# Head of a transformer block on Trainium2: conditioning groups summed on TensorE as columns, and the first projection units begun inside the head

## The chip, the cores and the metric

The kernel runs on one core of one Trainium2 chip. The metric is the device time of the whole kernel in microseconds (us). A core has TensorE (PE; its weight loads are shown as PEld), VectorE (DVE), ScalarE (ACT), GpSimd (POOL) and SyncE (SP), which here only issues DMAs. The engines run their own instruction streams and wait for one another on semaphores.

## The reference

The block has two sub-layers. What is touched here is the very beginning of the first one. Shapes: x is (512, 1024), c is (1, 1024), w_ada is (1024, 6144), w_in is (1024, 9 thousand odd columns), all float32.

```python
ada = (jax.nn.silu(c) @ w_ada[l] + b_ada[l])[:, None, :]
shift1, scale1, gate1, shift2, scale2, gate2 = jnp.split(ada, ADA_PARTS, axis=-1)
h = rms_norm(x, g_pre_mix[l]) * (1.0 + scale1) + shift1
# hybrid_mixer begins with one projection, whose first columns are convolved
proj = h @ w_in
m_qk = jax.nn.silu(causal_depthwise_conv(m_qk, conv_w, conv_b))
...
x = x + gate1 * rms_norm(y, g_post_mix[l])
# sub-layer 2: product-key retrieval over 16384 experts
```

## The kernel before, in words

All matrix products are done with a weight matrix split into two parts, a rounded part (`whi`, type fp32r) and the rest (`wlo`), and the activations too (`hi`, `lo`), three products for each pair. `h` is kept transposed: 8 slices k of 128 channels by 512 tokens.

**The head** (`head_block`, lines 143 to 374) makes `hi` and `lo` of the first sub-layer. It needs the first 2048 columns of `silu(c) @ w_ada` (shift1 and scale1). They come in 8 column groups of 256 columns, 1 MB each, in 4 pairs p: group p (shift) and group 4 + p (scale); each pair serves two slices k = 2p and 2p + 1. Groups 0 to 3 are summed by TensorE (`dot_columns`, line 248): silu(c) is the stationary operand of one column, the weights are the moving one of 256 columns, and the result is one row, which ACT copies out of PSUM (line 308) and TensorE turns into two columns (`turn_columns`, line 264). Groups 4 to 7 are summed by DVE in 8 steps (`ada_columns`, lines 135 and 138) and then turned by TensorE in the same way (line 264). A float32 matmul appears as two records in the trace, a transpose as one. Then DVE adds the bias (line 352) and makes the scale (line 356), ACT writes h and `hi` of both slices from the transposed x (lines 314 and 316, two instructions for each slice), and DVE writes `lo` (line 336). x itself is squared and summed by ACT (line 300), normalised by DVE (line 331) and transposed by TensorE (line 270, four transposes for each slice). The DMA queue of SP carries, in this order: small rows, x (2 MB), more small rows, the eight w_ada groups, and two groups of w_in (`load_ahead`, line 395).

Engines take their work strictly in program order, and the order is written out by hand. A block ends when all engines have finished it.

**The first projection** (`project_block`, called as "proj_m") runs over 18 groups of 256 weight columns. For a group, DVE casts the raw weights to `whi` (line 561), POOL subtracts to get `wlo` (line 488) and TensorE makes two units of 128 columns by 512 tokens, each 8 slices times 3 products = 24 matmuls (line 534). The very first group is an exception: its `whi` and `wlo` are made by DVE in four pieces at the start of the block (lines 579 and 581), and its first unit follows piece by piece. DVE convolves each of the first 16 units (lines 686 and 691), four instructions for a unit, and it casts the weights for the next group in between. Units of the later sections are emptied by ACT or DVE. SP loads groups two ahead, as soon as the raw buffer is free (line 451).

Of the kernel before, what the change touches and what calls it, by code (L numbers as in the profile page):

```python
# [79 lines left out]
HBUF = 4  # L80

# [37 lines left out]
def as_f32(ap):  # L119
    return ap.bitcast(F32)  # L120
# [22 lines left out]
def head_block(nc, con, slots, A, x_src, hi, lo):  # L143
# [3 lines left out]
    pairs_of, by_pe = [(p, KD // 2 + p) for p in range(KD // 2)], (0, 1, 2, 3)  # L147
    order = [g for pair in pairs_of for g in pair]

    with Alloc(nc, "head") as al:  # L150
# [7 lines left out]
        row = [al.sb(f"row{i}", [1, GC]) for i in range(2)]  # L158
# [4 lines left out]
        ps_t = al.ps("ps_t", [P, 512])  # L163
        ps_row = [al.ps(f"ps_row{i}", [P, 512]) for i in range(2)]
        ps_u = ps_l = ps_t
        ps_ada = al.ps("ps_ada", [P, 512])
# [6 lines left out]
        x_in = [al.sem(f"x_in{i}") for i in range(NT // 2)]  # L173
        acc_step, summed_up, ada_done, scale_done, lam_in, lam_prod, lam_sum, lam_exp, lam_done = map(
            al.sem, ("acc_step", "summed_up", "ada_done", "scale_done", "lam_in", "lam_prod", "lam_sum", "lam_exp",
                     "lam_done"))
        summed, meaned, powed, normed, turned, modded, hi_done, lo_done, row_done, row_kept = map(
            al.sem, ("summed", "meaned", "powed", "normed", "turned", "modded", "hi_done", "lo_done", "row_done",
                     "row_kept"))
        in_turn = [g for g in order if g in by_pe]  # L180
        row_turned = [order.index(g) + 1 for g in in_turn]
        block = al.block()

        @block.sync
        def _(sp):
            def rows(dst, r, src, n, sem):
                sp.dma_start(dst[r:r + n, :], src.rearrange("(r p) -> r p", p=P)).then_inc(sem, 16)

            rows(rows_a, R_BADA, A["b_ada"][0], 48, rows_in)
            rows(rows_a, R_GPREMIX, A["g_pre_mix"][0], 8, rows_in)  # L190
            rows(rows_a, R_GPOSTMIX, A["g_post_mix"][0], 8, rows_in)
            rows(rows_a, R_GPREFFN, A["g_pre_ffn"][0], 8, rows_in)
            rows(rows_a, R_GPOSTFFN, A["g_post_ffn"][0], 8, rows_in)
            rows(rows_a, R_CONVB, A["conv_b"][0], 16, rows_in)
            rows(rows_a, R_C, A["c"][0], 8, rows_in)
            for t in range(NT):
                sp.dma_start(x[:, t], x_src[t * P:(t + 1) * P, :]).then_inc(x_in[t // 2], 16)
            rows(rows_b, R_CONVW, A["conv_w"][0].rearrange("w c -> (w c)"), 64, rows_b_in)
            rows(rows_b, R_MGAIN, A["m_head_gain"][0], 8, rows_b_in)
            rows(rows_b, R_DGAIN, A["d_head_gain"][0], 8, rows_b_in)  # L200
            for n, name in enumerate(("lam_q1", "lam_q2", "lam_k1", "lam_k2")):
                sp.dma_start(con.lam_cols[:, n:n + 1], A[name].rearrange("a p -> p a")).then_inc(lam_in, 16)

            for n in range(2):
                sp.dma_start(con.gate_bias[:, n:n + 1],
                             A["b_if"][:, n * HEADS:(n + 1) * HEADS].rearrange("a h -> h a")).then_inc(lam_in, 16)
            for g in order[:-2]:
                sp.dma_start(raw[:, g], A["w_ada"][g].rearrange("p (k n) -> p k n", k=KD)).then_inc(landed[g], 16)
            for half, sems in enumerate(([landed[g] for g in order[-2:]], late)):
                ks = slice(half * KD // 2, (half + 1) * KD // 2)  # L210
                for g, sem in zip(order[-2:], sems):
                    src = A["w_ada"][g].rearrange("p (k n) -> p k n", k=KD)[:, ks]
                    sp.dma_start(raw[:, g, ks], src).then_inc(sem, 16)
            slots.load_ahead(sp, w_group(A["w_in"][0], C_QK))

        @block.gpsimd
        def _(pool):
# [13 lines left out]
            pool.tensor_tensor(rstd[:], ms[:], con.pow_half[:, 0:NT], ALU.pow).then_inc(powed, 1)  # L231
        @block.tensor
        def _(pe):
            pe.wait_ge(consts, 7)
            pe.wait_ge(rows_in, 112)
            pe.transpose(ps_t[:, 0:NROWS_A], rows_a[:], con.ident[0:NROWS_A, 0:NROWS_A]).then_inc(a_turned, 1)

            vec = [g for g in order if g not in by_pe]

            def dot_columns(g):  # L240

                i = in_turn.index(g)
                pe.wait_ge(landed[g], 16)
                wait(pe, row_kept, i - 1)
                for k in range(KD):
                    if k == KD // 2 and g in order[-2:]:
                        pe.wait_ge(late[order[-2:].index(g)], 16)
                    mm = pe.matmul(ps_row[i % 2][0:1, 0:GC], con.silu_c[:, k:k + 1], raw[:, g, k, :], start=(k == 0),
                                   stop=(k == KD - 1))
                mm.then_inc(row_done, 1)  # L250

            def turn_columns(g):

                if g in by_pe:
                    i = in_turn.index(g)
                    pe.wait_ge(row_kept, i + 1)
                    src, one, inner = row[i % 2], con.ones[0:1, 0:1], slice(0, 1)
                else:
                    i = vec.index(g)
                    pe.wait_ge(acc_step, KD * (i + 1))  # L260
                    src, one, inner = acc[i % 2], con.ones[:, 0:1], slice(0, P)
                for m in range(GC // P):
                    c = g * GC // P + m
                    mm = pe.matmul(ps_ada[:, c:c + 1], src[inner, m * P:(m + 1) * P], one, start=True, stop=True)
# [9 lines left out]
            for p, pair in enumerate(pairs_of):  # L274
                if p == 1:
                    pe.wait_ge(rows_b_in, 48)
                    pe.transpose(ps_u[:, 0:NROWS_B], rows_b[:], con.ident[0:NROWS_B, 0:NROWS_B]).then_inc(b_turned, 1)
                if p == 2:
                    pe.wait_ge(lam_prod, 1)
                    pe.wait_ge(cols_ready, 2)  # L280
                    pe.matmul(ps_l[:, 0:2], con.ones[:], sq[:], start=True, stop=True).then_inc(lam_sum, 1)
                for g in pair:
                    if g in by_pe:
                        dot_columns(g)
                if p == 0:
                    pe.wait_ge(normed, NT)
                for k in (2 * p, 2 * p + 1):
                    turn(k)
                for g in pair:
                    turn_columns(g)  # L290
        @block.scalar
        def _(act):
            act.wait_ge(cols_ready, 1)
            act.activation(con.silu_c[:], con.cols_a[:, R_C:R_C + KD], ACT.Silu).then_inc(silu_ready, 1)
            for t in range(NT):
                act.wait_ge(x_in[t // 2], 32)
# [4 lines left out]
            n_pe = 0  # L301
            for p, pair in enumerate(pairs_of):
                for g in pair:
                    if g in by_pe:
                        act.wait_ge(row_done, n_pe + 1)
                        if n_pe >= 2:
                            act.wait_ge(summed_up, row_turned[n_pe - 2])
                        act.activation(row[n_pe % 2][:], ps_row[n_pe % 2][0:1, 0:GC], ACT.Copy).then_inc(row_kept, 1)
                        n_pe += 1
# [8 lines left out]
                if p == 2:  # L318
                    act.wait_ge(lam_sum, 1)
                    act.activation(esum[:], ps_l[:, 0:2], ACT.Exp).then_inc(lam_exp, 1)  # L320

        @block.vector
        def _(dve):
# [6 lines left out]
            for t in range(NT):  # L330
# [2116 lines left out]
```

## Time and profile before

| | us |
|---|---|
| median of 3 runs | 2013.84 |
| lowest and highest | 2013.56, 2015.16 |
| span of the profiled execution | 2011.3 |

| engine | busy us | share of the span |
|---|---|---|
| PE | 1937.0 | 96% |
| DVE | 1489.4 | 74% |
| ACT | 719.0 | 36% |
| POOL | 481.5 | 24% |

The span runs from the first to the last instruction; what lies around it makes the 2.5 us to the median. Idle time of an engine that is not the bottleneck costs nothing; what an engine waited for is put down to the releaser that came last. PEclk is the TensorE clock that was granted, 1.00 for 2.4 GHz and 0.50 for 1.2 GHz. Matmuls are pipelined, so one record can be longer than the distance to the next one.

### The profile page before, as it was taken

What the parts mean: (1) busy time and instruction counts of PE and PEld (TensorE: products, weight loads), DVE (VectorE), ACT (ScalarE), POOL (GpSimd) and SP (SyncE); (2) the same over time, 40 slices, a digit from 0 to 9 for tenths busy, and PEclk for the clock granted to TensorE, in tenths of its full rate; (3) what the DMA queues carried; (4) which work ended last, traced back from release to release, by engine and by line L of the source; (5) the groups of instructions that cost most, each with busy time, mean ns of one, the idle gap of its engine ahead of it and who ended that gap; (6) DMA issues with size and microseconds to landing.
All of it is one profiled execution on the core that took longest, in us unless ns stands there. A gap on an engine that the chain in (4) does not pass through costs nothing.

```text
span 2011.3 us, 27895 instructions
## 1 busy us (share of the span) xinstructions
PE 1937.0 (96%) x10341; PEld 1714.5 (85%) x10341; DVE 1489.4 (74%) x2727; ACT 719.0 (36%) x1324; POOL 481.5 (24%) x240
## 2 busy tenths in 40 slices
PE   5999998999999989999999999999999999999998
PEld 3889776889877888899999999999988888888886
DVE  5677445364475545787889999997689889899895
ACT  4110234010252243344443444444444444444443
POOL 0443202343213113100111521111222323332221
PEclk9999999999999999999999999999999999999999
DMA  6335511354212422257767688888999999999993
GB/s 253 105 106 182 172 54 48 106 191 147 63 43 73 158 80 88 72 173 255 234 225 241 231 318 297 299 296 300 412 395 401 401 400 398 400 398 401 400 375 115
DMA packets 212642, 467.99 MB, mean 233 GB/s; under 512 B 13576, under 2 KB 157120, under 8 KB 193344
## 3 DMA queue, kind: packets, MB, share of 16 engines
q1 hardware_dynamic: 194112, 332.54, 47.6%
q0 software_dynamic: 18432, 134.23, 16.9%
q8 instruction: 51, 0.84, 0.2%
q14 instruction: 47, 0.39, 0.1%
HBM read 412.19 MB, written 54.53 MB: 232 GB/s over the span
## 4 chain that ended last, share of the span: by engine, by line
PE 52%; DVE 2%; DMA 2%; ACT 1%; issue 0%; POOLq 0%; POOL 0%; SPq 0%; ACTq 0%; DVEq 0%
PE xin_out L2038 26%; PE xin_ps_u L1994 22%; PE xin_out L2016 4%; DMA con_raw<-in_expert_u 2%; DVE in_ulo L2156 1%; ACT in_uhi L2067 0%; DVE experts_rows L1787 0%; DVE experts_acc L1806 0%; DVE over_s_stage L2170 0%; ACT L2109 0%; ACT over_v_vhi L2074 0%; DVE over_v_vlo L2305 0%; POOLq L95 0%; POOL xin_x L2147 0%; DVE over_s_stage L2253 0%
## 5 line engine op out<-in xcount | busy, mean ns | idle before, releaser
L1780 POOL DMA_INDIRECT experts_rows<-in_expert_rows,experts_idx x128 | 247.3, 1932 | 873.2 <-DVE experts_acc L1806 738.4
L1994 PE MATMUL xin_ps_u<-con_h_hi,in_uhi 128*128 128x384 f32 x1024 | 349.0, 341 | 9.4 <-DVE in_ulo L2156 7.2
L1994 PE MATMUL xin_ps_u<-con_h_hi,in_ulo 128*128 128x384 f32 x1024 | 343.3, 335 | 0.0
L1994 PE MATMUL xin_ps_u<-con_h_lo,in_uhi 128*128 128x384 f32 x1024 | 343.3, 335 | 0.0
L2038 PE MATMUL xin_out<-over_v_vhi,xin_whi 128*128 128x512 f32 x768 | 239.1, 390 | 2.1 <-DVE xin_wlo L2307 2.0
L2038 PE MATMUL xin_out<-over_v_vhi,xin_wlo 128*128 128x512 f32 x768 | 238.8, 390 | 0.0
L2038 PE MATMUL xin_out<-over_v_vlo,xin_whi 128*128 128x512 f32 x768 | 238.5, 390 | 0.0
L2156 DVE TENSOR_TENSOR in_ulo<-con_raw,in_uhi 128x1024 fp32r<-128x1024 f32 x127 | 155.5, 1224 | 78.3 <-ACT in_uhi L2067 75.9
L488 POOL TENSOR_TENSOR weights_wlo<-con_raw,weights_whi 128x2048 fp32r<-128x2048 f32 x32 | 147.5, 4609 | 251.9 <-DVE weights_whi L561 251.9
L1994 PEld LDWEIGHTS xin_ps_u<-con_h_hi,in_uhi 128*128 128x128 f32 x1024 | 193.1, 189 | 13.7 <-DVE in_ulo L2156 11.1
L1994 PEld LDWEIGHTS xin_ps_u<-con_h_lo,in_uhi 128*128 128x128 f32 x1024 | 193.2, 189 | 0.0
L1994 PEld LDWEIGHTS xin_ps_u<-con_h_hi,in_ulo 128*128 128x128 f32 x1024 | 192.7, 188 | 0.0
L2038 PEld LDWEIGHTS xin_out<-over_v_vhi,xin_whi 128*128 128x128 f32 x768 | 144.0, 188 | 33.4 <-DVE over_v_vlo L2305 2.7
L2074 ACT ACTIVATE over_v_vhi<-con_raw 128x1024 fp32r<-128x1024 f32 x128 | 135.0, 1055 | 103.8 <-DMA con_raw<-in_expert_v 88.6
L2092 ACT ACTIVATE in_act<-xin_ps_u 128x384 f32<-128x384 f32 x128 | 62.9, 491 | 300.2 <-PE xin_ps_u L1994 300.2
L2038 PEld LDWEIGHTS xin_out<-over_v_vhi,xin_wlo 128*128 128x128 f32 x768 | 144.3, 188 | 29.9
L2038 PEld LDWEIGHTS xin_out<-over_v_vlo,xin_whi 128*128 128x128 f32 x768 | 144.3, 188 | 29.7
L2305 DVE TENSOR_TENSOR over_v_vlo<-con_raw,over_v_vhi 128x1024 fp32r<-128x1024 f32 x128 | 156.4, 1222 | 9.1 <-ACT over_v_vhi L2074 8.8
L1806 DVE SCALAR_TENSOR_TENSOR experts_acc<-experts_rows,experts_coef,experts_acc 128x1024 f32<-128x1024 f32 x127 | 162.8, 1282 | 0.1
L1787 DVE SCALAR_TENSOR_TENSOR experts_rows<-experts_rows,con_h 128x1024 f32<-128x1024 f32 x128 | 156.3, 1221 | 0.1
L2067 ACT ACTIVATE in_uhi<-con_raw 128x1024 fp32r<-128x1024 f32 x127 | 133.9, 1054 | 9.3 <-DMA con_raw<-in_expert_u 9.0
L2076 ACT ACTIVATE xin_whi<-xin_wt 128x384 fp32r<-128x384 f32 x128 | 67.2, 525 | 177.7 <-DVE xin_wt L2302 177.2
(344 smaller groups left out, 3742.4 us busy)
## 6 DMA issues: line engine op xcount, KB each, us to landing
con_raw<-in_expert_u SPq DMA_DIRECT2D x128, 512.0 KB, 4.7
con_raw<-in_expert_v SPq DMA_DIRECT2D x128, 512.0 KB, 12.0
con_raw<-in_w_in SPq DMA_DIRECT2D x38, 1024.0 KB, 6.0
act_scratch<-in_act SPq DMA_DIRECT2D x128, 192.0 KB, 2.4
experts_hot<-act_scratch SPq DMA_DIRECT2D x128, 192.0 KB, 11.8
gate_scratch<-in_stage SPq DMA_DIRECT2D x12, 1024.0 KB, 7.1
gate_scratch<-over_s_stage SPq DMA_DIRECT2D x12, 1024.0 KB, 7.7
experts_hot<-gate_scratch SPq DMA_DIRECT2D x16, 768.0 KB, 14.1
```

The costliest lines, as they stand in the source:

```text
L488: pool.tensor_tensor(wlo[s][:], raw[s][:], as_f32(whi[s][:]), ALU.subtract).then_inc(w_lo, 1)
L1780: pool.indirect_dma_start(out=self.rows[:, r % ROWS, :], out_offset=None, in_=table, in_offset=at).then_inc(self.row_in[r % ROWS], 16)
L1787: dve.scalar_tensor_tensor(out=u, in0=u, scalar=1.0, in1=h0, op0=ALU.mult, op1=ALU.mult, accum_out=self.dots[:, r:r + 1]).then_inc(self.do ...
L1806: dve.scalar_tensor_tensor(out=self.acc[:], in0=v, scalar=self.coef[:, r:r + 1], in1=self.acc[:], op0=ALU.mult, op1=ALU.add).then_inc(self ...
L1994: mm = pe.matmul(ps_u[s % 2][:, 0:TD], a[s % 2][:, k, :], m[:, k, P:T], start=(i == 0), stop=(i == 3 * KD - 1))
L2016: mm = pe.matmul(ps_g[b][:, k, :], hot_j[q % 2][:, 4 * b + k, :], hot_i[q % 2][:, 4 * b + k, :], start=True, stop=True)
L2038: product = lambda s, t, h, w, m, **flags: pe.matmul(out[t][h][:], w[s][:, t * P:(t + 1) * P], m[s][:, h * 512:(h + 1) * 512], **flags)
L2067: act.activation(uhi[n % 2][:], cut_of[n % U_RING], ACT.Copy).then_inc(hi_done, 1)
L2074: act.activation(vhi[s][:], v[s], ACT.Copy).then_inc(vhi_done, 1)
L2076: act.activation(whi[s][:], wt[n % 2][:], ACT.Copy).then_inc(whi_done, 1)
L2156: dve.tensor_tensor(ulo[n % 2][:], cut_of[n % U_RING], as_f32(uhi[n % 2][:]), ALU.subtract).then_inc(lo_done, 1)
L2305: dve.tensor_tensor(vlo[s][:], v[s], as_f32(vhi[s][:]), ALU.subtract).then_inc(vlo_done, 1)
```

## The change

- `dots(p)` takes the place of `dot_columns` and of the turning of its row: the raw weights (128 x 128) are the stationary operand and one column of silu(c) the moving one; 2 column blocks by 8 slices = 16 matmuls for a group (32 records), straight into columns of PSUM. ACT's copies of the rows (line 308) go.
- The loads: w_ada group 0 goes ahead of x; the first w_in group goes ahead of the last pair of w_ada; the second w_in group stays last. Small rows, lambda columns and gate biases are issued on ACT's queue instead of SP's (three before silu, six behind it). x is waited for tile by tile.
- x: DVE normalises two of the four tiles, ACT the other two. TensorE transposes slices 0 to 3 at once, then 4 and 5, then 6 and 7.
- Both first w_in groups are split in the head: `whi` by ACT (`split_hi`), `wlo` by DVE (`split_lo`), group 0 between pairs 2 and 3, group 1 at the very end. The four-piece split at the start of proj_m goes, and so do DVE's cast and POOL's subtraction of group 1.
- `begin`: units 0 and 1 are begun in the head's two first PSUM banks, with 7 of 8 slices (42 of 48 matmuls), as far as `lo` is done. Four slices of unit 0 stand ahead of `turn_columns(3)` on TensorE. proj_m only adds slice 7.

```diff
+BEGUN, BEGUN_K = 2, 7
...
         @block.sync
...
+            column_group(PAIRS_OF[0][0])
             for t in range(NT):
-                sp.dma_start(x[:, t], x_src[t * P:(t + 1) * P, :]).then_inc(x_in[t // 2], 16)
...
+                sp.dma_start(x[:, t], x_src[t * P:(t + 1) * P, :]).then_inc(x_in[t], 16)
+            column_group(PAIRS_OF[0][1])
+            for pair in PAIRS_OF[1:LAST]:
+                for g in pair:
+                    column_group(g)
+            sp.dma_start(slots.raw[0][:], load_in(sp, 0, 0)).then_inc(slots.landed[0], 16)
+            for half, sems in enumerate(([landed[g] for g in PAIRS_OF[LAST]], late)):
...
+            sp.dma_start(slots.raw[1][:], load_in(sp, 0, 1)).then_inc(slots.landed[1], 16)
...
         @block.tensor
...
-                    mm = pe.matmul(ps_row[i % 2][0:1, 0:GC], con.silu_c[:, k:k + 1], raw[:, g, k, :], start=(k == 0),
-                                   stop=(k == KD - 1))
...
+            def dots(p):
...
+                        mm = pe.matmul(ps_ada[p % 2][:, c:c + 1], raw[:, g, k, m * P:(m + 1) * P],
+                                       con.silu_c[:, k:k + 1], start=(k == 0), stop=(k == KD - 1))
+                mm.then_inc(dotted, 1)
...
+            def begin(c, ks):
+
+                cs = slice(c * P, (c + 1) * P)
+                for k in ks:
+                    pe.wait_ge(lo_done, k + 1)
+                    for n, (a, m) in enumerate(((slots.whi, hi), (slots.whi, lo), (slots.wlo, hi))):
+                        pe.matmul(bank[c][:], a[0][:, k, cs], m[:, k, :], start=(k == 0 and n == 0), stop=False)
+
             pe.wait_ge(silu_ready, 1)
...
+            dots(0)
...
+            pe.wait_ge(normed, NT // 2)
+            pe.wait_ge(act_normed, NT // 2)
+            for k in range(4):
+                turn(k)
+            turn_columns(0)
+            dots(1)
+            turn_columns(1)
...
+            for k in (4, 5):
+                turn(k)
+            dots(2)
+            turn_columns(2)
+            for k in (6, 7):
+                turn(k)
+            dots(3)
+            pe.wait_ge(lam_exp, 1)
+            pe.wait_ge(w_lo, 1)
+            begin(0, range(0, 4))
+            turn_columns(3)
+            begin(1, range(0, 4))
+            for ks in (range(4, 6), range(6, BEGUN_K)):
+                for c in range(BEGUN):
+                    begin(c, ks)
...
         @block.scalar
...
+            act.wait_ge(powed, 1)
+            for t in range(NT // 2, NT):
+                act.activation(x[:, t], x[:, t], ACT.Copy, scale=rstd[:, t:t + 1]).then_inc(act_normed, 1)
+
+            def split_hi(s):
+                act.wait_ge(slots.landed[s], 16)
+                act.activation(slots.whi[s][:], slots.raw[s][:], ACT.Copy).then_inc(w_hi, 1)
+
+            for p in range(LAST + 1):
+                if p == 2:
+                    act.wait_ge(lam_sum, 1)
+                    act.activation(esum[:], ps_l[:, 0:2], ACT.Exp).then_inc(lam_exp, 1)
+                    split_hi(0)
                 act.wait_ge(scale_done, p + 1)
...
+            split_hi(1)
...
         @block.vector
...
+            def split_lo(s):
+                dve.wait_ge(w_hi, s + 1)
+                dve.tensor_tensor(slots.wlo[s][:], slots.raw[s][:], as_f32(slots.whi[s][:]),
+                                  ALU.subtract).then_inc(w_lo, 1)
...
+            sums(1)
+            scales(1)
+            for k in (0, 1):
+                low(k)
+            sums(2)
+            scales(2)
+            for k in (2, 3):
+                low(k)
+            split_lo(0)
+            sums(3)
+            scales(3)
+            for k in (4, 5):
+                low(k)
...
+            for k in (6, 7):
+                low(k)
+            split_lo(1)
+    return bank
...
-def project_block(nc, tag, slots, sections, make, ada=None, following=None, split_first=False):
+def project_block(nc, tag, slots, sections, make, ada=None, following=None, begun=None):
...
-        before = 0 if split_first else 1
-        bank = [al.ps(f"bank{i}", [P, 512]) for i in range(4)]
...
+        before = 2 if begun else 1
+        home = [al.ps(f"bank{i}", [P, 512]) for i in range(4)]
+        bank = begun + home[BEGUN:] if begun else home
...
+                            if begun and opening and s == 0:
+
+                                ks = range(BEGUN_K, KD)
...
-                dve.tensor_copy(whi[0][:, part], raw[0][:, part]).then_inc(hi_sem, 1)
...
-                dve.tensor_tensor(wlo[0][:, part], raw[0][:, part], as_f32(whi[0][:, part]),
-                                  ALU.subtract).then_inc(lo_sem, 1)
```

## Rows read from the trace of the kernel before

**Rows 1.** The page: busy time of each engine, and the chain that ended last.

```profile
PE 1937.0 (96%) x10341; PEld 1714.5 (85%) x10341; DVE 1489.4 (74%) x2727; ACT 719.0 (36%) x1324; POOL 481.5 (24%) x240
PE 52%; DVE 2%; DMA 2%; ACT 1%; issue 0%; POOLq 0%; POOL 0%; SPq 0%; ACTq 0%; DVEq 0%
```

**Rows 2.** Busy us in three stretches: PE, PEld, DVE, ACT, POOL, PEclk, DMA, GB/s.

```profile
42.00:46.00 4.00, 0.00 (x0) 0.00 (x0) 2.73 (x6) 2.93 (x5) 0.00 (x0) 0.50 0.00 0
46.00:52.00 6.00, 4.90 (x12) 3.85 (x13) 5.23 (x9) 1.13 (x1) 0.55 (x1) 0.50 0.11 13
...
18.00:38.00 20.00, 18.43 (x105) 10.24 (x104) 15.91 (x43) 9.00 (x15) 0.00 (x0) 1.00 0.99 372
```

**Rows 3.** Timeline, end of the head: start us, us, engine, line, what, [idle before].

```profile
41.79 0.16 DVE L356 SCALAR_TENSOR_TENSOR con_scale_a<-con_ada,con_cols_a 128x2 f32<-128x2 f32 x1
...
43.99 0.78 ACT L316 ACTIVATE con_h_hi<-head_ps,con_ada,con_scale_a 128x512 fp32r<-128x512 f32 x1
44.87 0.69 DVE L336 TENSOR_TENSOR con_h_lo<-head_h,con_h_hi 128x512 fp32r<-128x512 f32 x1 [0.64 <-ACT con_h_hi L316]
...
45.89 0.43 DVE L579 CAST weights_whi<-con_raw 128x512 fp32r<-128x512 f32 x1 [0.33 <-PEq L95]
...
47.10 0.79 PE L534 MATMUL proj_m_bank<-con_h_hi,weights_whi 128*128 128x512 f32 x1 [5.60 <-DVE weights_wlo L581]
```

**Rows 4.** Timeline, x and the first pair of groups in the head.

```profile
12.58 1.06 ACT L300 ACTIVATE head_junk<-head_x 128x1024 f32<-128x1024 f32 x1
...
14.31 5.35 PE L248 MATMUL head_ps_row<-head_raw,con_silu_c 128*1 128x256 f32 x16 [9.25 <-DMA head_raw<-in_w_ada]
...
15.16 2.74 DVE L331 TENSOR_SCALAR head_x<-head_x,head_rstd 128x1024 f32<-128x1024 f32 x4 [1.15 <-POOL head_rstd L231]
...
18.20 3.61 DVE L138 SCALAR_TENSOR_TENSOR head_acc<-head_raw,con_silu_c,head_acc 128x256 f32<-128x256 f32 x7
...
21.86 0.61 PE L264 MATMUL head_ps_ada<-con_ones,head_acc 128*128 128x1 f32 x4 [0.64 <-DVE head_acc L138]
...
22.77 0.16 DVE L356 SCALAR_TENSOR_TENSOR con_scale_a<-con_ada,con_cols_a 128x2 f32<-128x2 f32 x1
```

**Rows 5.** Groups by line in the head: count, busy us, mean ns.

```profile
L264 PE MATMUL head_ps_ada<-con_ones,head_acc 128*128 128x1 f32 x16 | 2.4, 256 | 0.7 <-DVE head_acc L138 0.6
```

**Rows 6.** Timeline of PE: four transposes twice; and a stretch's granted clock.

```profile
336.71 0.66 PE L880 MATMUL mlstm_ps_t<-con_ident,mlstm_cell 128*128 128x128 f32 x4 [1.14 <-DVE mlstm_cell L957]
338.66 1.05 PE L880 MATMUL mlstm_ps_t<-con_ident,mlstm_cell 128*128 128x128 f32 x4 [1.30 <-DVE mlstm_tmp L963]
...
339.00:340.00 1.00, 0.71 (x4) 0.31 (x2) 0.25 (x1) 0.18 (x1) 0.00 (x0) 0.50 0.00 0
```

**Rows 7.** PE at matmuls of four rows, and the stretch behind them.

```profile
255.90 3.70 PE L834 MATMUL mlstm_ps_n<-mlstm_g,con_sel 4*128 4x512 f32 x8
...
260.30:263.50 3.20, 3.20 (x5) 1.17 (x4) 0.80 (x2) 3.17 (x5) 0.29 (x1) 0.50 0.00 0
```

**Rows 8.** Groups by line of the whole kernel: operations on 128x2048 elements.

```profile
L488 POOL TENSOR_TENSOR weights_wlo<-con_raw,weights_whi 128x2048 fp32r<-128x2048 f32 x32 | 147.5, 4609 | 251.9 <-DVE weights_whi L561 251.9
...
L2233 DVE TENSOR_TENSOR over_s_stage<-over_s_stage 128x2048 f32<-128x2048 f32 x8 | 18.3, 2285 | 0.0
...
L1738 ACT ACTIVATE weights_whi<-con_raw 128x2048 fp32r<-128x2048 f32 x7 | 13.4, 1913 | 2.8 <-PEq L95 1.5 <-DMA con_raw<-in_w_query 1.3
```

**Rows 9.** DMA from 0 to 42 us in 40 slices, and SP's issue of w_in.

```profile
GB/s 0 23 12 16 203 367 417 351 414 346 238 421 421 414 414 437 398 460 414 421 437 414 445 406 414 367 277 250 414 409 381 378 344 352 347 227 33 13 8 0
...
14.21 14.18 SPq L395 DMA_DIRECT2D con_raw<-in_w_in  x2
```

**Rows 10.** Timeline of DVE in proj_m: two convolutions' first steps, a cast between.

```profile
60.61 0.81 DVE L686 TENSOR_SCALAR proj_m_acc<-proj_m_bank,con_cols_b,con_cols_a 128x512 f32<-128x512 f32 x1 [2.27 <-PE proj_m_bank L534]
...
63.70 1.22 DVE L561 CAST weights_whi<-con_raw 128x2048 fp32r<-128x2048 f32 x1
66.05 0.81 DVE L686 TENSOR_SCALAR proj_m_acc<-proj_m_bank,con_cols_b,con_cols_a 128x512 f32<-128x512 f32 x1 [1.14 <-PE proj_m_bank L534]
```

More of the change, by code:

```diff
@@ L143, in head_block @@
 def head_block(nc, con, slots, A, x_src, hi, lo):
-    pairs_of, by_pe = [(p, KD // 2 + p) for p in range(KD // 2)], (0, 1, 2, 3)
-    order = [g for pair in pairs_of for g in pair]
+    PAIRS_OF, LAST = [(p, KD // 2 + p) for p in range(KD // 2)], KD // 2 - 1
+    w_ada_of = lambda g: A["w_ada"][g].rearrange("p (k n) -> p k n", k=KD)
     with Alloc(nc, "head") as al:
@@ L200, in _ @@
[L200 to L208, printed above, removed]
@@ L209, in _ @@
-            for half, sems in enumerate(([landed[g] for g in order[-2:]], late)):
+            rows(sp, rows_a, R_BADA, A["b_ada"][0], 48, rows_in)
+            rows(sp, rows_a, R_GPREMIX, A["g_pre_mix"][0], 8, rows_in)
+            rows(sp, rows_a, R_GPOSTMIX, A["g_post_mix"][0], 8, rows_in)
+            rows(sp, rows_a, R_GPREFFN, A["g_pre_ffn"][0], 8, rows_in)
+            rows(sp, rows_a, R_GPOSTFFN, A["g_post_ffn"][0], 8, rows_in)
+            rows(sp, rows_a, R_CONVB, A["conv_b"][0], 16, rows_in)
@@ L210, in _ @@
+            sp.dma_start(slots.raw[0][:], load_in(sp, 0, 0)).then_inc(slots.landed[0], 16)
+            for half, sems in enumerate(([landed[g] for g in PAIRS_OF[LAST]], late)):
                 ks = slice(half * KD // 2, (half + 1) * KD // 2)
[L211 to L214, printed above, removed]
+                for g, sem in zip(PAIRS_OF[LAST], sems):
+                    sp.dma_start(raw[:, g, ks], w_ada_of(g)[:, ks]).then_inc(sem, 16)
@@ L236, in _, with turn_columns @@
             pe.transpose(ps_t[:, 0:NROWS_A], rows_a[:], con.ident[0:NROWS_A, 0:NROWS_A]).then_inc(a_turned, 1)
-            vec = [g for g in order if g not in by_pe]
-            def dot_columns(g):
-                i = in_turn.index(g)
+            def dots(p):
+                g = PAIRS_OF[p][0]
                 pe.wait_ge(landed[g], 16)
[L244 to L247, printed above, removed]
-                    mm = pe.matmul(ps_row[i % 2][0:1, 0:GC], con.silu_c[:, k:k + 1], raw[:, g, k, :], start=(k == 0),
-                                   stop=(k == KD - 1))
[L250 to L261, printed above, removed]
-                for m in range(GC // P):
-                    c = g * GC // P + m
-                    mm = pe.matmul(ps_ada[:, c:c + 1], src[inner, m * P:(m + 1) * P], one, start=True, stop=True)
+                if p >= 2:
+                    pe.wait_ge(ada_done, 2 * (p - 1))
+                for m in range(GC // P):
+                    for k in range(KD):
+                        if p == LAST and m == 0 and k == KD // 2:
+                            pe.wait_ge(late[0], 16)
+                        c = g * GC // P + m
+                        mm = pe.matmul(ps_ada[p % 2][:, c:c + 1], raw[:, g, k, m * P:(m + 1) * P],
+                                       con.silu_c[:, k:k + 1], start=(k == 0), stop=(k == KD - 1))
+                mm.then_inc(dotted, 1)
+            def turn_columns(p):
+                pe.wait_ge(acc_step, KD * (p + 1))
+                for m in range(GC // P):
+                    c = PAIRS_OF[p][1] * GC // P + m
+                    mm = pe.matmul(ps_ada[p % 2][:, c:c + 1], acc[p % 2][:, m * P:(m + 1) * P], con.ones[:, 0:1],
+                                   start=True, stop=True)
                 mm.then_inc(summed_up, 1)
@@ new lines, in _ @@
+            pe.wait_ge(cols_ready, 2)
+            pe.matmul(ps_l[:, 0:2], con.ones[:], sq[:], start=True, stop=True).then_inc(lam_sum, 1)
+            for k in (4, 5):
[13 more added lines that the diff above has]
+                    begin(c, ks)
@@ L497, in _ @@
                     for s in range(2):
-                        very_first = isinstance(it, int) and gb + 2 * it + s == 0
-                        if not very_first:
+                        opening = isinstance(it, int) and gb + 2 * it + s < before
+                        if not opening:
                             pe.wait_ge(w_lo, gb + 2 * it + s + 1 - before)
@@ L550, in view @@
                         last_group = isinstance(it, int) and gb + 2 * it + s + 1 == g0
[L551 removed]
+                        ready = isinstance(it, int) and gb + 2 * it + s + 1 < before
+                        if eng is nc.vector and not ready and (following or not last_group):
                             o = 1 - s
```

159 lines of the change are left out of this document (55 added, 104 removed).

## The prediction, on record before the change was run

> **What bounds the kernel now.** I read the page's busy line first: TensorE is busy for 96% of the span, and the chain that ended last is nearly all TensorE [rows 1]. So a change at the very start is worth exactly what it shifts the moment from which TensorE runs without a gap. The busy time by stretch shows where that is: from 42 to 46 us TensorE does nothing, and from 46 to 52 it does 12 matmuls in 4.9 us at a granted clock of 0.50 [rows 2], 0.41 for each. The timeline names the gap: the last scale is done at 41.95, ACT's last `hi` at 44.77, DVE's last `lo` at 45.56, the next block's first DVE cast starts 0.33 later and the first matmul at 47.10 [rows 3]. Units then end every 5.44 us, 0.2267 for each of 24 matmuls (66.05 - 60.61 [rows 10]), so unit 1 ends at 60.5 and group 2 starts two units later, at 71.4. That time is the measure; behind it the same work follows in the same order. The whole head is a loop of DVE: sums, wait for TensorE's turning, scale, `lo`.
>
> **The start of the chain.** Group 0 (1 MB) ahead of x delays x by some 2.6 us at about 400 GB/s [rows 9]; but x is now squared tile by tile, and its last square, until now at 13.64 [rows 4], ends at about 14.9. The normalising then starts at 16.4 instead of 15.16. DVE does two tiles instead of four (1.4 of 2.74 us), so its first sum starts at 17.8, as before, and ends at 21.8. ACT's two tiles take 2 x 1.06, until 18.5, and the 16 transposes behind them end by 22 even at the slow pace. `dots(0)` lies in the wait for x. So the first scale is done at 22.9, as before [rows 4]: no gain, no loss. ACT's nine small DMA issues (some 0.4 us each, an estimate from SP's pace) lie before the first x tile lands at about 9; without that cover each would cost its 0.4.
>
> **DVE's loop.** From the end of a sum to the end of its scale is 1.1 us (21.81 to 22.93 [rows 4]); a sum is 4.0, a `lo` 0.69 but 0.65 in a row [rows 3], a whole-group `wlo` 2.3, a `whi` on ACT 1.9 (the same shapes elsewhere [rows 8]).
> - scale 1: 22.9 + 0.65 (four small instructions near 0.16) + 4.0 + 1.1 = 28.7
> - scale 2: + 1.3 + 4.0 + 1.1 = 35.1
> - scale 3: + 1.3 + 2.3 (`split_lo(0)`) + 4.0 + 1.1 = 43.8, where 41.95 stood before
> - end of the head: + 2.8 (ACT's four instructions, 41.95 to 44.77 [rows 3]) + 1.9 (`split_hi(1)`) + 2.3 (`split_lo(1)`) = 50.8, where 45.56 stood.
>
> So the head gets 5.2 us longer, 2.3 + 1.9 + 2.3 of it for splits and less for the rest. What it buys is 42 matmuls, 9.5 us at 0.2267, done in `begin`, and the slow start of the clock taken there.
>
> **Behind the head.** Slice 7 for both units is 6 matmuls, 1.4 us, then group 1 takes 10.9: TensorE would be at group 2 at 50.8 + 0.45 + 12.3 = 63.5. But its weights come later: DVE must convolve units 0 and 1 first (3.1 each, 60.61 to 63.70), cast (1.2 [rows 10]), then POOL subtracts (4.6 [rows 8]): 1.3 + 6.2 + 1.2 + 0.1 + 4.6 = 13.5 after the head, 64.3. TensorE waits 0.8 there; later groups have their slack again, as DVE has 7.5 us of work in each 10.9. Against 71.4 this is **-7.1 us**, if TensorE is at full clock all the time.
>
> **TensorE's clock decides the rest.** `dots(p)` has 32 records. Turning an accumulator is the same form: 4 records in 0.61 us, the last of them 0.256 long, so 0.12 apart [rows 4, 5]; a group costs about 3.7 us at full clock, against 16 x 0.21 = 3.4 before. At the low clock four transposes took 1.05 where they took 0.66 before [rows 6], nearly 0.21 against 0.11 apart; I take 7.1 us for cold `dots`. The clock starts low (the first 16 records took 5.35 us instead of 3.6 [rows 4]) and falls when little streams: after eight matmuls of 512 columns but only 4 rows, back to back for 3.7 us, the granted clock was 0.50 [rows 7]. TensorE was busy there all the time, so being busy isn't enough. It also fell at the end of the head, behind transposes and matmuls of one column, before TensorE had idled long: 0.50 at 42 [rows 2]. The old dots stream 256 columns and held it; the new ones stream one and load weights. So I expect it to fall in `dots`.
>
> The Trainium skill ("TensorE: Matmul & The Clock Gate", "LDWEIGHTS (loading the stationary operand)") gives a weight load's time as columns over 1.2 GHz, the same at either clock. By it cold `dots` would stay at 3.4 us, an estimate from that page, and the sum would be about -6 us. The trace disagrees: transposes with loads of 128 columns came 0.21 apart instead of 0.11 at the low clock [rows 6].
>
> - All slow in `begin`'s first 12 matmuls alone: `wlo` of group 0 is there at 38.7; 12 x 0.42 = 5.0, to 43.7; `turn_columns(3)` stands behind them, though its sum ended at 42.7; scale 3 at 44.8, head's end 51.8, group 2 at 65.3: **-6.1**.
> - `dots(3)` slow too: `turn_columns(2)` ends at 34.7, two slow turns to 36.4, dots to 43.5, `begin` to 48.5, scale 3 at 50.0, head's end 57.0, group 2 at 70.5: **-0.9**. With half of it slow -3.6.
> - `dots(1)` and `dots(2)` slow as well: they begin at 22.9 and end at 30.0, scale 1 at 31.5; turns 4 and 5 to 33.0, dots to 40.1, scale 2 at 41.6; turns and dots to 49.8, `begin` to 54.8, scale 3 at 56.3, head's end 63.3: group 2 at 76.8, **+5.4**.
>
> The bursts of transposes (16, 8 and 8) stream fully and may raise the clock again between the dots, so I take the middle: some dots slow, most of `dots(3)` and `begin`'s start slow, about **-3 us**. That is the step with the widest bounds, -7.1 to +5.4.
>
> **Other parts.** ACT's row copies (4 x 0.37 us) and the turning of rows go; both stood beside DVE's sums, worth nothing. On SP the second w_in issue had blocked its queue (two issues in 14.18 us [rows 9]) while the DMA engines stayed full; now the last pair of w_ada stands behind one w_in issue. It is needed at 38.7 and lands, by the sum of megabytes ahead, at about 35; the first w_in group lands at about 29.5 and ACT comes to it at 33 (behind the mods of pair 1, 2.8, and a table load, 1.3). Cover of 3.8 and 3.5 us; if a load is later than that, each further us costs one. ACT's exponential and `split_hi(0)` stand ahead of the mods of pair 2, which need scale 2 at 35.1; ACT is done with the split at about 35.0: no wait, but no slack either; a late w_in group would hold `hi` of slices 4 and 5, not the chain of DVE before scale 3.
>
> **Rivals.**
> - A, the dots keep 0.12 a record: the clock stays up in them (the transposes' streaming suffices, or weight loads count), or, with 0.03 of the chance, weight loads of 128 columns keep their pace at the low clock: -5.5 to -7.1 us, say 2007.4. For it: from 18 to 38 us the clock stood at 1.00, turnings of one column in every pair [rows 2]. Against: the fall at 42 us, and the transposes' pace for the second [rows 6].
> - B, the clock falls in part: -4.2 to -0.9; taken at -3.0.
> - C, slower than before: cold dots put TensorE in place of DVE as what ends last in each pair. 7.1 + 1.7 + 1.5 us of TensorE against 6.4 of DVE, 2.7 to 3.9 lost in each of three pairs. Break-even is a head that ends at 57.9, or scale 3 at 50.9; with all dots cold +5.4, 2019.2.
> - D, the change doesn't do what it says: a late load (or a longer queue at ACT) holds the sums, and the begun units only fill a gap that the longer head opened: within 1 us of before.
>
> **How the numbers follow.** The profiled execution has 2011.3 for 2013.84 in the median, 2.5 around it; a shift of the start moves both alike, and the clock's falls later on (each some 1 to 2 us) come out a little otherwise each time. Chances: B 0.50, A 0.30, C 0.12, D 0.08. Prediction: 2013.84 - 3.0 = 2010.8. Range: A's -7.1 to C's +5, so 2006.6 to 2018.0. About 0.2%, 4.0 us, is what a measurement can tell from no change: faster is A and the edge of B, 0.37; slower C's upper part and some of D, 0.12; the same 0.51.
>
> **What would show it.** The profile after should have scale 0 at about 23, scale 1 at 29 to 31, scale 2 at 35 to 40, scale 3 at 44 to 52; 32 records of `dots` in 3.7 us or in 7; the granted clock at 0.50 within `dots(2)`, `dots(3)` or the start of `begin`; DVE's last `wlo` about 7 us behind scale 3; a wait of about 1 us of TensorE for POOL ahead of group 2. I am wrong if sums wait for DMA, if weight loads of one-column matmuls are slower than 0.12 apart at full clock, or if the time behind group 2 doesn't move with it.

## The result, and the profile after

| | before | after |
|---|---|---|
| median of 15 runs each, us | 2014.87 | 2020.38 |
| lowest and highest, us | 2011.78, 2021.3 | 2015.0, 2025.75 |
| span of the profiled execution, us | 2011.3 | 2015.9 |

The ratio is 1.0023, with an interval from 1.0015 to 1.0032: the kernel after is slower, by 4.6 us by the ratio and by 5.5 between the medians, where 3 us faster was forecast. 2020.4 lies above the range.

The busy line of the page after, to be read beside that of before [rows 1]. TensorE is busy 11 us longer, and its weight loads 21 us longer:

```profile
PE 1948.2 (97%) x10389; PEld 1735.8 (86%) x10389; DVE 1485.1 (74%) x2718; ACT 723.4 (36%) x1324; POOL 442.6 (22%) x239
```

The stretches of after (busy us of PE, PEld, DVE, ACT, POOL, then PEclk, DMA share and GB/s):

```profile
20.00:26.00 6.00, 6.00 (x45) 6.00 (x44) 4.82 (x16) 1.98 (x3) 0.00 (x0) 1.00 1.01 419
27.00:47.00 20.00, 19.38 (x93) 19.30 (x93) 13.95 (x30) 8.82 (x11) 0.00 (x0) 0.50 0.54 194
47.40:53.00 5.60, 5.60 (x16) 4.44 (x16) 0.00 (x0) 0.00 (x0) 0.00 (x0) 0.50 0.00 0
54.00:60.00 6.00, 6.00 (x28) 4.96 (x27) 4.01 (x7) 4.59 (x5) 0.00 (x0) 1.00 0.01 3
```

The gap of TensorE that [rows 2] showed from 42 to 46 is gone: it is busy for 19.38 of the 20 us from 27 to 47. But all of that is at a granted clock of 0.50 (1.2 GHz), which lasts from 26.1 to 53.4 us. In the trace of before the clock stood at 1.00 until 41.8, when the last scale was being made. The 1.00 in the row from 20 to 26 holds only from about 22.7 on: the profile has no clock record before that, and the pace of the transposes (16 in 3.37 us, from 19.75) is that of the low clock.

The timeline of TensorE after:

```profile
8.42 6.96 PE L246 MATMUL head_ps_ada<-con_silu_c,head_raw 128*128 128x1 f32 x32 [3.28 <-DMA head_raw<-in_w_ada]
...
19.75 3.37 PE L262 MATMUL head_ps<-con_ident,head_x 128*128 128x128 f32 x16 [4.14 <-ACT head_x L325]
...
23.32 4.43 PE L246 MATMUL head_ps_ada<-con_silu_c,head_raw 128*128 128x1 f32 x32
...
29.67 1.95 PE L262 MATMUL head_ps<-con_ident,head_x 128*128 128x128 f32 x8
31.41 6.83 PE L246 MATMUL head_ps_ada<-con_silu_c,head_raw 128*128 128x1 f32 x32
38.10 0.99 PE L255 MATMUL head_ps_ada<-con_ones,head_acc 128*128 128x1 f32 x4
38.95 1.95 PE L262 MATMUL head_ps<-con_ident,head_x 128*128 128x128 f32 x8
40.69 6.83 PE L246 MATMUL head_ps_ada<-con_silu_c,head_raw 128*128 128x1 f32 x32
47.38 0.77 PE L271 MATMUL head_bank<-con_h_hi,weights_whi 128*128 128x512 f32 x1
...
52.64 0.85 PE L255 MATMUL head_ps_ada<-con_ones,head_acc 128*128 128x1 f32 x4
...
61.29 0.47 PE L564 MATMUL head_bank<-con_h_hi,weights_whi 128*128 128x512 f32 x1 [0.83 <-PEq L96]
...
74.37 0.50 PE L564 MATMUL head_bank<-con_h_hi,weights_whi 128*128 128x512 f32 x1 [0.58 <-POOL weights_wlo L521]
```

The `dots` of pairs 2 and 3 (31.41 and 40.69) take 6.83 us each, those of pair 1 took 4.43 because the clock was up for a short while, until 26.1. From 28.4 on the work follows without a gap: turning, transposes, dots, begun units. The last row is group 2 of proj_m, the measure of the prediction: 74.37, where the trace of before has it at 71.29. The last scale, on DVE:

```profile
53.59 0.23 DVE L377 TENSOR_TENSOR con_ada<-head_ps_ada,con_cols_a 128x2 f32<-128x2 f32 x2 [6.59 <-PE head_ps_ada L255]
53.86 0.16 DVE L381 SCALAR_TENSOR_TENSOR con_scale_a<-con_ada,con_cols_a 128x2 f32<-128x2 f32 x1
```

DVE waited 6.59 us for TensorE's turning. Before, TensorE's turning waited for DVE's sum [rows 4]; now DVE waits for TensorE. In the rest of the kernel the lag against before's trace is 1.7 to 3.3 us up to 610 us and 4.8 from 660 on; it changes where a fall of the clock comes out otherwise, mostly by 1.5 to 1.7 us at a time.

### The profile page after: what moved, and what is told of

It reads as the page before. It is cut to its first block, busy times and chain, and to the rows that moved or that the text cites. A ratio compares the mean times of both kernels' runs of the same rounds, so it can differ in the third digit from the quotient of the medians.

```text
span 2015.9 us, 27980 instructions
## 1 busy us (share of the span) xinstructions
PE 1948.2 (97%) x10389; PEld 1735.8 (86%) x10389; DVE 1485.1 (74%) x2718; ACT 723.4 (36%) x1324; POOL 442.6 (22%) x239
## 4 chain that ended last, share of the span: by engine, by line
PE 52%; DVE 2%; DMA 2%; ACT 1%; issue 0%; POOLq 0%; POOL 0%; SPq 0%; ACTq 0%; DVEq 0%
PE xin_out L2061 26%; PE xin_ps_u L2017 22%; PE xin_out L2039 4%; DMA con_raw<-in_expert_u 2%; DVE in_ulo L2179 1%; ACT in_uhi L2090 0%; DVE experts_rows L1810 0%; ACT L2132 0%; DVE experts_acc L1829 0%; DVE over_s_stage L2193 0%; ACT over_v_vhi L2097 0%; POOLq L96 0%; DVE over_v_vlo L2328 0%; POOL xin_x L2170 0%; DVE over_s_stage L2276 0%
## 5 line engine op out<-in xcount | busy, mean ns | idle before, releaser
L1803 POOL DMA_INDIRECT experts_rows<-in_expert_rows,experts_idx x128 | 213.0, 1664 | 905.1 <-DVE experts_acc L1829 768.6
L521 POOL TENSOR_TENSOR weights_wlo<-con_raw,weights_whi 128x2048 fp32r<-128x2048 f32 x31 | 142.8, 4607 | 258.8 <-DVE weights_whi L592 258.8
L2061 PEld LDWEIGHTS xin_out<-over_v_vhi,xin_wlo 128*128 128x128 f32 x768 | 144.2, 188 | 30.1
L2061 PEld LDWEIGHTS xin_out<-over_v_vlo,xin_whi 128*128 128x128 f32 x768 | 144.2, 188 | 29.8
```

Source lines behind the costliest of these rows:

```text
L521: pool.tensor_tensor(wlo[s][:], raw[s][:], as_f32(whi[s][:]), ALU.subtract).then_inc(w_lo, 1)
L1803: pool.indirect_dma_start(out=self.rows[:, r % ROWS, :], out_offset=None, in_=table, in_offset=at).then_inc(self.row_in[r % ROWS], 16)
L2061: product = lambda s, t, h, w, m, **flags: pe.matmul(out[t][h][:], w[s][:, t * P:(t + 1) * P], m[s][:, h * 512:(h + 1) * 512], **flags)
```

## The experiments

Two theories. **Clock**: the one-column matmuls leave TensorE at 1.2 GHz, and this costs the whole gain and more. **Order and splits**: the longer head (two splits, the wait of `turn_columns(3)` behind begun units) costs it, and the clock is a side matter. Names with a_ are variants of the kernel after, names with b_ of the kernel before. None leaves out part of the computation.

**a_wide**: the same number of matmuls and weight loads, but each streams the column of silu(c) 128 times, and DVE reads one of the 128 equal results.

```diff
-                        mm = pe.matmul(ps_ada[p % 2][:, c:c + 1], raw[:, g, k, m * P:(m + 1) * P],
-                                       con.silu_c[:, k:k + 1], start=(k == 0), stop=(k == KD - 1))
+                        mm = pe.matmul(ps_ada[p % 2][:, P + m * 128:P + (m + 1) * 128], raw[:, g, k, m * P:(m + 1) * P],
+                                       con.silu_c[:, k:k + 1].to_broadcast([P, 128]), start=(k == 0), stop=(k == KD - 1))
```

> The changed kernel, with one edit: the one column of silu(c) that the dots stream is read 128 times (128 equal columns out, one is used). Matmul and weight load counts are the same. Clock theory (the dots stream so little that the clock falls, and the head was slow for that alone): the granted clock stays at 1.00 from about 20 us on, 32 records of dots take 3.5 to 3.7 us instead of 6.9, scale 3 is done at 45 to 46 instead of 54.0, group 2 begins at 65 to 67 instead of 74.4, and the kernel is 7 to 9 us faster than the changed one, 3 to 6 us faster than before. Rival (the splits moved into the head, and the wait behind the begun units, cost more than is begun): the dots get faster at most, group 2 begins at 72 or later, the kernel stays slower than before. Third (streaming 128 columns costs TensorE time of its own): dots take 7 us or more at a clock of 1.00.

Measured: 0.9982 of before (0.9972 to 0.9993), 2011.55 us beside 2015.3. It is faster than both kernels, by a small step that is clear of the noise. Its stretches and TensorE's timeline:

```profile
27.00:47.00 20.00, 17.94 (x131) 16.25 (x131) 16.58 (x38) 11.21 (x16) 0.00 (x0) 1.00 0.54 194
47.40:53.00 5.60, 4.72 (x22) 3.60 (x21) 3.04 (x3) 3.00 (x3) 0.00 (x0) 1.00 0.02 3
```

```profile
30.26 3.74 PE L246 MATMUL head_ps_ada<-con_silu_c,head_raw 128*128 128x128 f32 x32
...
36.35 3.74 PE L246 MATMUL head_ps_ada<-con_silu_c,head_raw 128*128 128x128 f32 x32
...
43.55 0.60 PE L255 MATMUL head_ps_ada<-con_ones,head_acc 128*128 128x1 f32 x4 [0.74 <-DVE head_acc L139]
...
65.05 0.50 PE L565 MATMUL head_bank<-con_h_hi,weights_whi 128*128 128x512 f32 x1 [0.57 <-POOL weights_wlo L522]
```

The clock is at 1.00 from 25.5 on, the dots of pairs 2 and 3 take 3.74 instead of 6.83 us although each streams 128 times as much, turning waits for DVE again, and group 2 starts at 65.05: 9.3 us earlier than after, 6.2 earlier than before. The splits and the order are the same as in after, so they aren't what made it slower.

**a_row**: the dots in before's form (silu stationary, 256 columns of weights streamed, ACT copies the row), all else as after.

```diff
-                        mm = pe.matmul(ps_ada[p % 2][:, c:c + 1], raw[:, g, k, m * P:(m + 1) * P],
-                                       con.silu_c[:, k:k + 1], start=(k == 0), stop=(k == KD - 1))
+                    mm = pe.matmul(ps_ada[p % 2][0:1, GC:2 * GC], con.silu_c[:, k:k + 1], raw[:, g, k, :],
+                                   start=(k == 0), stop=(k == KD - 1))
...
+                act.activation(row[p % 2][:], ps_ada[p % 2][0:1, GC:2 * GC], ACT.Copy).then_inc(row_kept, 1)
```

> The changed kernel with the summing by TensorE undone: silu(c) is the stationary column again, 256 weight columns stream, ACT copies the row and TensorE turns it. All else (loads, splits, begun units) stays. Clock theory: clock at 1.00 from about 17 to 20 us on, dots 3.4 us, group 2 at 66 to 68, 3 to 5 us faster than before. Rival (splits and order cost): group 2 at 72 or later, slower than before.

Measured: 0.999 (0.9977 to 1.0003), 2012.62 us; dots 5.82, 3.61, 4.49 and 3.61 us, the clock at 0.50 only to 23.3 and from 30.1 to 33.5; group 2 at 67.30, 4.0 before before's. So the loads, splits and begun units of the change bring the start of group 2 forward with before's dots too; only the column form with one column doesn't. Two things came out below the expectation: the time isn't told apart from before's, and the clock wasn't at 1.00 throughout from 20 us on. It fell once more behind the turning of pair 1, with 256 columns streamed in all dots.

**a_turnfirst**: `turn_columns(3)` ahead of the begun units.

```diff
+            turn_columns(3)
             pe.wait_ge(lam_exp, 1)
             pe.wait_ge(w_lo, 1)
             begin(0, range(0, 4))
-            turn_columns(3)
```

> The changed kernel with turn_columns(3) ahead of the first begun slices of unit 0. Clock theory: scale 3 is done at about 49.3 instead of 54.0, but TensorE still has 42 matmuls from 48.2 on, the first dozen or more at the low clock, so the head ends within 0.7 us of where it did and the kernel within 1 us of the changed one. Rival (the wait behind the begun units sets the head's end): the head ends 4 to 5 us earlier, the kernel is 4 to 5 us faster than the changed one.

Measured: 1.0013 (0.9999 to 1.0026), 2015.83 us. The last scale ended at 48.79 instead of 54.02, 5.2 us earlier, but group 2 only at 73.71 instead of 74.37. DVE's last `wlo` ended at 55.74, while TensorE was still in the begun units until 60.3: with the clock at 0.50 until 53.3, TensorE's own work sets the end, and where the turning stands in it matters little. The head behaved as expected, the kernel's time didn't: its median is 4.5 us below that of after, which is the size that the rival had named. But the two intervals overlap, so the medians don't tell the kernels apart, and group 2 starts only 0.7 us earlier; the rest of the 3.8 us between the two spans (2012.1 and 2015.9) comes behind the head, where the clock's falls come out otherwise.

**a_nobegin**: no begun units (`BEGUN_K = 0`, and no calls of `begin`, so `turn_columns(3)` follows `dots(3)`); proj_m makes all 8 slices.

```diff
-BEGUN, BEGUN_K = 2, 7
+BEGUN, BEGUN_K = 2, 0
```

> The changed kernel without begun units: all 48 matmuls of units 0 and 1 in proj_m, turn_columns(3) right behind dots(3). Both first weight groups are still split in the head. Clock theory, with begun units worth what they fill: head's end at 56 to 57 instead of 61, group 2 at 79 to 82, 5 to 7 us slower than the changed kernel. Rival (the begun units cost as much as they give, since they run at the low clock anyway): within 2 us of the changed one.

Measured: 1.0073 (1.0054 to 1.0092), 2029.23 us; dots 6.96, 6.96, 6.83, 6.83 us; group 2 at 82.5, 8.2 us later than after, and the median 8.9 above after's, where 5 to 7 were expected. Not all of it is the begun units': here `dots(1)` was slow from its start (6.96 beside 4.43 us), so scale 2 ended at 41.95 instead of 39.61. From scale 2 to group 2 it takes 40.6 us and after 34.8, so the begun units are worth 5.8 us at the low clock.

**b_cols and b_wide**: the kernel before with only the form of the dots changed: b_cols streams 1 column, b_wide 128 equal ones. Order, loads and splits are before's.

```diff
-                    mm = pe.matmul(ps_row[i % 2][0:1, 0:GC], con.silu_c[:, k:k + 1], raw[:, g, k, :], start=(k == 0),
-                                   stop=(k == KD - 1))
+                        mm = pe.matmul(ps_row[i % 2][:, m * 1:(m + 1) * 1], raw[:, g, k, m * P:(m + 1) * P],
+                                       con.silu_c[:, k:k + 1], start=(k == 0), stop=(k == KD - 1))
```

> The kernel before with one part of the change alone: groups 0 to 3 summed by TensorE straight into columns (weights stationary, one column of silu(c) streamed); no row, no copy by ACT, no turning of it. Loads, splits and the start of proj_m as before. Clock theory: the clock is at 0.50 in most of the dots, 32 records take 6.8 to 7.0 us; TensorE's part of a pair (dots, two transposed slices, turning) is up to 9.7 us where the pair took 6.3 to 6.9; scale 3 at 46 to 54 instead of 41.95, the kernel 5 to 11 us slower than before. Rival (the summed form is harmless, the slowdown is from splits and order): within 2 us of before.

> As the one before, but with silu(c)'s column streamed 128 times. Clock theory: clock at 1.00 from about 20 to 41 us, dots 3.5 to 3.7 us, scale 3 within 1 us of 41.95, the kernel within 2 us of before. Rival: as slow as with one column.

Measured: b_cols 1.0074 (1.0058 to 1.009), 2032.14 us; b_wide 0.9995 (0.9986 to 1.0003), 2014.47 us. b_cols, TensorE's timeline:

```profile
43.98 6.96 PE L247 MATMUL head_ps_row<-con_silu_c,head_raw 128*128 128x1 f32 x32
50.80 1.95 PE L266 MATMUL head_ps<-con_ident,head_x 128*128 128x128 f32 x8
...
59.07 0.80 PE L524 MATMUL proj_m_bank<-con_h_hi,weights_whi 128*128 128x512 f32 x1 [5.68 <-DVE weights_wlo L571]
```

and the same of b_wide:

```profile
34.40 3.82 PE L247 MATMUL head_ps_row<-con_silu_c,head_raw 128*128 128x128 f32 x32
38.06 1.03 PE L266 MATMUL head_ps<-con_ident,head_x 128*128 128x128 f32 x8
...
47.02 0.80 PE L524 MATMUL proj_m_bank<-con_h_hi,weights_whi 128*128 128x512 f32 x1 [5.67 <-DVE weights_wlo L571]
```

One edit, the width of the stream, moves the first matmul of proj_m from 47.02 to 59.07 (before: 47.10 [rows 3]) and the median by 17.7 us, more than the 5 to 11 that were expected of b_cols. In b_cols the clock's records begin late and the column PEclk reads 1.00 until then; the pace tells the clock there, 8 transposes in 1.95 us beside 1.03. Of the 17.7 us, 12.05 are in the head, which one pair of traces shows; in b_cols the lag behind before's trace grew later, from 11.3 us at 233 to 20 at 1477. That part was not followed up.

With the theory of the clock shown, four more runs measured what the pieces are worth: two start from a_wide, two mix narrow and wide dots.

**a_wide_xfirst**: x ahead of w_ada group 0 in SP's queue.

```diff
-            column_group(PAIRS_OF[0][0])
             for t in range(NT):
                 sp.dma_start(x[:, t], x_src[t * P:(t + 1) * P, :]).then_inc(x_in[t], 16)
+            column_group(PAIRS_OF[0][0])
```

> The changed kernel with the 128 equal columns, and x ahead of w_ada group 0 in the queue again. In the run with group 0 ahead, scale 0 was done at 24.3 us against 22.9 before. If the load order costs that: scale 0 at 22.9 to 23.3, every later scale and group 2 about 1.0 to 1.4 us earlier (group 2 at about 64), the kernel 1 us faster than with group 0 ahead. Rival (dots(0), which then start at 14.3, stand in the way of the transposes): scale 0 at 24 or later, no gain.

Measured: 0.9974 (0.9964 to 0.9985), 2010.59 us, the lowest median of all, though not told apart from a_wide. In the head the rival came true and nothing moved: scale 0 at 24.45 (a_wide 24.28) and group 2 at 65.22. x comes earlier, but the transposes don't:

```profile
15.09 6.66 PE L246 MATMUL head_ps_ada<-con_silu_c,head_raw 128*128 128x128 f32 x32 [10.03 <-DMA head_raw<-in_w_ada]
...
21.66 1.91 PE L262 MATMUL head_ps<-con_ident,head_x 128*128 128x128 f32 x16
```

`dots(0)`, at the low clock of the start, now stands ahead of them until 21.7.

**a_wide_nobegin**: a_wide with `BEGUN_K = 0`.

> The changed kernel with the 128 equal columns and without begun units; both first weight groups still split in the head. Begun units at full clock fill a gap and keep the clock: without them TensorE idles from 44 to 52, the clock falls, 48 matmuls take 13 to 15 us, group 2 at 75 to 78 instead of 65.05, 9 to 12 us slower than with them. Rival (the gain of the version with 128 columns comes from the splits and the dots, not from the begun units): within 3 us of it.

Measured: 1.0038 (1.0024 to 1.0053), 2022.65 us, 11 us above a_wide; group 2 at 76.8, as expected. TensorE has nothing to do at the head's end, and the clock is at 0.50 from 43.8 to 57.4, so proj_m starts slowly on top of having more to do. The longer head pays only with the begun units. The wide dots of pair 2 took 5.18 us here, as the clock was at 0.50 from 30.1 to 33.5.

**a_wide_last and a_wide_but_last**: 128 columns in `dots(3)` alone, and in all but `dots(3)`. The edit of a_wide_last is shown; a_wide_but_last has `p < LAST` in place of `p == LAST`.

```diff
+                        W = P if p == LAST else 1
+                        mm = pe.matmul(ps_ada[p % 2][:, P + m * P:P + m * P + W], raw[:, g, k, m * P:(m + 1) * P],
+                                       con.silu_c[:, k:k + 1].to_broadcast([P, W]), start=(k == 0), stop=(k == KD - 1))
```

> The changed kernel with 128 equal columns in dots(3) alone; dots(0) to (2) stream one column. Question: how much of the 9.3 us between the two versions lies in the dots, how much in the begun units that start slowly behind them. If a slow dots(3) hands its clock to the begun units: scale 2 still at 39.6, dots(3) slow at first but the clock up within them, first 12 begun matmuls in 3 us instead of 5.3, scale 3 at 48 to 50 instead of 54.0, group 2 at 69 to 71 instead of 74.4, 3 to 5 us faster than the changed kernel. Rival (the dots of pairs 1 and 2 cost it): group 2 at 73 or later.

> The changed kernel with 128 equal columns in dots(0) to (2) and one column in dots(3) alone. If the last dots cost most: scale 2 at 36 as with 128 columns everywhere, the clock falls within dots(3) or right behind, the begun units start at 0.50 at 40 to 43, scale 3 at 46 to 49 instead of 44.7, group 2 at 67 to 70 instead of 65.05. Rival (the dots of pairs 1 and 2 cost it): group 2 within 1 us of 65.05.

Measured: a_wide_last 1.002 (1.0009 to 1.003), 2019.25 us, group 2 at 71.79; a_wide_but_last 0.9984 (0.9971 to 0.9996), 2011.13 us, group 2 at 66.11. TensorE's timeline of a_wide_last:

```profile
23.91 6.97 PE L247 MATMUL head_ps_ada<-con_silu_c,head_raw 128*128 128x1 f32 x32
...
33.75 6.83 PE L247 MATMUL head_ps_ada<-con_silu_c,head_raw 128*128 128x1 f32 x32
...
43.03 4.76 PE L247 MATMUL head_ps_ada<-con_silu_c,head_raw 128*128 128x128 f32 x32
```

and of a_wide_but_last:

```profile
29.41 1.08 PE L263 MATMUL head_ps<-con_ident,head_x 128*128 128x128 f32 x8
30.32 5.37 PE L247 MATMUL head_ps_ada<-con_silu_c,head_raw 128*128 128x128 f32 x32
...
36.80 3.63 PE L247 MATMUL head_ps_ada<-con_silu_c,head_raw 128*128 128x1 f32 x32
...
66.11 0.50 PE L566 MATMUL head_bank<-con_h_hi,weights_whi 128*128 128x512 f32 x1 [0.58 <-POOL weights_wlo L523]
```

In a_wide_last `dots(1)` was slow from its start, so its scales came later than in after (scale 2 at 41.96 instead of 39.61, where 39.6 was expected). Group 2 was expected at 69 to 71, and the median, 1.1 us below after's, isn't told apart from it. From scale 2 on it needs 29.8 us to group 2, after 34.8: the wide dots of the last pair bring the clock up at 45.2, and the begun units run at 0.24 us a matmul from their start. In a_wide_but_last a single group of one-column dots still ran at full speed, 3.63 us; the clock fell right behind it, until 44.1. Group 2 came 1.1 us later than in a_wide, between what the expectation and its rival had said, and only 0.6 of that belongs to the narrow dots: the wide dots of pair 2 took 5.37 us instead of 3.74, with the clock at 0.50 from 30.4 to 33.9, and scale 2 ended 0.45 us later. So 128 columns don't hold the clock in every execution. It isn't one group of such dots but their row of three with the low clock between them that makes the loss: each pair then waits for TensorE.

## Why the prediction was wrong, point by point

- **The step that failed** is the choice of B: "The bursts of transposes (16, 8 and 8) stream fully and may raise the clock again between the dots, so I take the middle". The two bursts of 8 don't: in after the clock stayed at 0.50 through both (29.67 and 38.95, 1.95 us each) and through 6 us of begun matmuls of 512 columns. The burst of 16 did, but for 3.4 us only, and not each time: in after and a_turnfirst `dots(1)` behind it took 4.43 and 4.48 us, in a_nobegin and a_wide_last, whose TensorE does the same up to there, 6.96 and 6.97. So `dots(2)` and `dots(3)` were slow from end to end, not in part. There was no row behind that sentence; [rows 7] and the fall at 42 us [rows 2] spoke for C.
- **Rival C** had the mechanism right, at a chance of only 0.12. Its all-cold working gave group 2 at 76.8; measured 74.37. `dots(1)` had its first 2.8 us at full clock (4.43 instead of 7.1 us). The other terms: scale 1 forecast 31.5, measured 29.9; scale 2 41.6 and 39.6; scale 3 56.3 and 54.0. After scale 1 each step is within 0.4 us, up to scale 3. Its 2019.2 was 1.2 us below the median of 2020.38, so it would have been the better forecast for the right reason. The stated range left it out: C's +5.4 is 2019.2, and even the +5 that the range names is 2018.8 and not 2018.0.
- **The price of the dots** was right: 7.1 at the low clock and 3.7 at full clock, measured 6.83 to 6.97 and 3.63. The pace came from the transposes at the two clocks [rows 6].
- By the Trainium skill ("TensorE: Matmul & The Clock Gate", "LDWEIGHTS (loading the stationary operand)") a load takes its columns over 1.2 GHz, one formula for both clocks. The runs disagree, with 6.83 us at the low clock and 3.63 at full clock for the same 32 records.
- **The full-clock chain** (-7.1, A) is what a_wide ran: -6.2. Scale 0 was mis-sized: it ended at 24.28 (in after at 23.98), not at 22.9, because x landed a microsecond later than I had worked out from the megabytes ahead of it: its last square started at 14.83 and not near 13.8, and the normalising at 17.41 and not at 16.4. ACT's and DVE's timelines of after:

```profile
14.83 1.06 ACT L322 ACTIVATE head_junk<-head_x 128x1024 f32<-128x1024 f32 x1 [0.19 <-DMA head_x<-in_x]
...
17.41 1.42 DVE L355 TENSOR_SCALAR head_x<-head_x,head_rstd 128x1024 f32<-128x1024 f32 x2 [1.15 <-POOL head_rstd L227]
```

  From scale 0 to scale 3 the forecast had 20.9 us and a_wide 20.4; from there to group 2 20.5 and 20.4.
- **The begun units' slow start**: forecast 5.0 us for 12 matmuls, in after 5.3 to the turning. It was there only behind narrow dots: in a_wide they ran at 0.23 each from the first on.
- **The wait of TensorE for POOL** at group 2: forecast 0.8, measured 0.58 in after and 0.57 in a_wide. The splits: 1.93 and 2.29 us, forecast 1.9 and 2.3. ACT's DMA issues and the loads: no sum and no dot of pairs 1 to 3 waited for a load, so D is out.
- **The step from the head to the median**: a shift of the start should move the median alike. Group 2 moved by +3.1, spans by 4.6, medians by 5.5. In a_wide group 2 moved by -6.2, the span by -3.0 and the median by -3.75. Two things on record bear on it. First, an execution with `dots(1)` slow throughout, as in a_nobegin and a_wide_last, has scale 2 at 41.95 (C's working: 41.6), 2.3 us behind the one trace of after; how many executions of after are like that isn't known. Second, b_wide has its group 2 where before has it (71.09 and 71.29) and its median 0.2 us below before's, and its traced span is still 3.4 us longer, so single traces differ by that much with nothing shifted in the head. It doesn't always go against the variant: in a_turnfirst group 2 moved by +2.4 and the span by +0.8. How the 5.5 us divide between these stays open.

## What to carry to other kernels

Here matmuls that stream one column behind a weight load of 128 kept TensorE busy for 19.38 of 20 us and left it at half its clock, and all that stood behind them on TensorE paid for that. Streaming the same column 128 times costs next to nothing in time (3.74 beside 3.63 us for 32 records) and held the clock through pair 2 in three traces of five with wide dots there (a_wide, a_wide_xfirst, b_wide); in the other two it fell once, which cost 0.4 us up to scale 2. Widths between 1 and 128 weren't run. Where a rival rests on rows and the forecast on a hope ("may raise the clock again"), give the rival the chance.

## What the runs showed of the hardware that was not expected

- 32 float32 records (16 matmuls) with loads of 128 columns take 3.63 us with 1 streamed column and 3.74 to 3.82 with 128, both at full clock; 6.83 to 6.97 us with 1 column at 0.50.
- Neither 8 transposes in 1.95 us nor the first 6 us of matmuls of 512 columns right behind one-column dots brought the clock back; in after it stayed down for 27.3 us in all.
- The same instructions didn't get the same clock each time: `dots(1)` behind 16 transposes took 4.43 and 4.48 us in two traces and 6.96 and 6.97 in two others.
- The wide dots brought the clock back: in a_wide_last it came up within `dots(3)`, at 45.2. They didn't always hold it: `dots(2)` with 128 columns took 5.18 us in a_wide_nobegin and 5.37 in a_wide_but_last, with the clock at 0.50 for 3.4 us.
